# The opening of a hybrid RG-LRU / gMLP layer: decay series a term a round, spills on GpSimd's queue, another order of factors, rows and samples

## The reference

```
ada = silu(c) @ w_ada + b_ada            # nine vectors of 1024 for each of 9 sequences
h = x + 0.5 * g1 * SwiGLU1(mod(rms(x)))
h = h + gm * Mixer(mod(rms(h)))          # causal conv + RG-LRU, and a gMLP gating unit
h = h + 0.5 * g2 * SwiGLU2(mod(rms(h)))
y = mod(rms(h)) with shift, scale = silu(c) @ w_ada_final + b_ada_final
mod(v) = v * (1 + scale) + shift         # per sequence
```

## Time and profile before

| | us |
|---|---|
| median of 3 runs | 2403.04 |
| lowest, highest | 2400.04, 2405.37 |
| the profiled execution | 2404.43 |
| its span in the profile | 2402.7 |
| PE, DVE, ACT busy | 2342.3, 1579.6, 985.2 |

### The profile page before, as it was taken

How to read it: one execution, slowest core, us unless ns; L and a number is a source line. 1 busy time by engine, 2 the same in 40 slices (tenths; PEclk the granted TensorE clock), 3 DMA queues, 4 the chain that set the end, 5 groups by cost and what they waited for, 6 DMA issues and landing times.

```text
span 2402.7 us, 31657 instructions
## 1 busy us (share of the span) xinstructions
PE 2342.3 (97%) x11530; PEld 2007.2 (84%) x11530; DVE 1579.6 (66%) x2530; ACT 985.2 (41%) x1701; POOL 129.7 (5%) x173
## 2 busy tenths in 40 slices
PE   6999999999999999999999999999999999999998
PEld 4677777787788787999999999997777788878887
DVE  5965665666666766655666565569666666666667
ACT  4544444444233443443344434235444444433335
POOL 0010101100000000101011110000010100000000
PEclk8999999999999999999999999999999999999998
DMA  9465455548855332321222213423645533497642
GB/s 347 158 202 179 159 178 189 165 164 302 341 214 187 130 125 89 120 57 45 65 65 62 61 38 112 150 81 102 210 158 177 186 129 127 159 379 276 236 140 82
DMA packets 247342, 381.02 MB, mean 159 GB/s; under 512 B 16689, under 2 KB 158185, under 8 KB 246070
## 3 DMA queue, kind: packets, MB, share of 16 engines
q1 hardware_dynamic: 234526, 345.15, 41.7%
q0 software_dynamic: 10240, 33.56, 4.5%
q10 hardware_dynamic: 2456, 0.75, 0.1%
HBM read 262.93 MB, written 116.47 MB: 158 GB/s over the span
## 4 chain that ended last, share of the span: by engine, by line
PE 83%; DVE 8%; DMA 3%; issue 2%; ACT 2%; SPq 0%; DVEq 0%; ACTq 0%
PE bank L535 25%; PE bank L537 24%; PE bank L536 24%; PE bank L2931 2%; PE bank L2928 2%; PE bank L2930 2%; DMA wraw<-in_w_ffn_down 2%; DVE u_lo L629 1%; PE bank L2814 1%; PE bank L2844 1%; DVE wraw L656 1%; DVE x L2263 1%; DVE x L1909 1%; DMA xrow<-in_x_prompt 1%; DMA wraw<-in_w_ffn_up 1%
## 5 line engine op out<-in xcount | busy, mean ns | idle before, releaser
L535 PE MATMUL bank<-ops,u_hi 128*128 128x512 f32 x1232 | 489.2, 397 | 9.2 <-DVE ops L1942 4.0
L629 DVE TENSOR_TENSOR u_lo<-wraw,u_hi 128x512 fp32r<-128x512 f32 (+2 forms) x532 | 315.4, 618 | 277.3 <-ACT u_hi L623 274.9
L537 PE MATMUL bank<-ops,u_lo 128*128 128x512 f32 x1232 | 482.0, 391 | 0.0
L536 PE MATMUL bank<-ops,u_hi 128*128 128x512 f32 x1232 | 481.6, 391 | 0.0
L623 ACT ACTIVATE u_hi<-wraw 128x512 fp32r<-128x512 f32 (+2 forms) x532 | 287.4, 568 | 278.0 <-PE bank L537 167.8
L535 PE MATMUL bank<-xn_hi,w_hi 128*128 128x384 f32 x1104 | 370.5, 336 | 5.2 <-ACT ww L1689 2.0
L537 PE MATMUL bank<-xn_hi,w_lo 128*128 128x384 f32 x1104 | 369.6, 335 | 0.0
L536 PE MATMUL bank<-xn_lo,w_hi 128*128 128x384 f32 x1104 | 369.4, 335 | 0.0
L535 PEld LDWEIGHTS bank<-ops,u_hi 128*128 128x128 f32 x1232 | 232.6, 189 | 86.4 <-issue 23.4
L537 PEld LDWEIGHTS bank<-ops,u_lo 128*128 128x128 f32 x1232 | 232.5, 189 | 49.7
L536 PEld LDWEIGHTS bank<-ops,u_hi 128*128 128x128 f32 x1232 | 232.8, 189 | 46.5
(11 more groups left out here) (320 smaller groups left out, 3959.0 us busy)
## 6 DMA issues: line engine op xcount, KB each, us to landing
h_dram<-stage_hi SPq DMA_DIRECT2D x154, 256.0 KB, 2.4
h_dram<-stage_lo SPq DMA_DIRECT2D x154, 256.0 KB, 2.7
ada_in<-in_w_ada POOLq DMA_DIRECT2D x96, 256.0 KB, 3.7
raw<-in_w_in SPq DMA_DIRECT2D x48, 512.0 KB, 4.8
wraw<-in_w_ffn_gate SPq DMA_DIRECT2D x44, 512.0 KB, 4.8
wraw<-in_w_ffn_up SPq DMA_DIRECT2D x44, 512.0 KB, 4.9
wraw<-in_w_ffn_down SPq DMA_DIRECT2D x48, 384.0 KB, 5.2
x<-x_dram SPq DMA_DIRECT2D x6, 2304.0 KB, 9.4
```

Of the source, the lines that this page charges most:

```text
L535: nc.tensor.matmul(out, hi, mov_hi, start=first, stop=False, skip_group_check=True)
L536: nc.tensor.matmul(out, hi, mov_lo, start=False, stop=False, skip_group_check=True)
L537: return nc.tensor.matmul(out, lo, mov_hi, start=False, stop=last, skip_group_check=True)
L629: nc.vector.tensor_tensor(unit(u_lo, f, g, u, n), unit_source(u, n), unit(u_hi, f, g, u, n).bitcast(F32), ALU.subtract).then_inc(u_lo_read ...
```

## The change

VectorE's decay series is cut in pieces: `decay_begins` after round 1 of the first FFN, one `decay_term` after each of rounds 2 to 8, `decay_ends` after round 9; its buffer `spw` moves to a place of its own. The four input spills leave SP's queue for POOL's (with semaphores `x_kept`), and so do the gate-block loads, from ScalarE's. SP loads x tiles 6 to 8 without waiting for a spill, and weights ahead of modulation half 2. `first_rows(0)` and the fold of half 0 stand ahead of x tiles 3 to 5, the square root for tiles 0 to 3 after the fourth tile's squares; the factor's spread goes to bank 7 and ahead of `first_half(1)`. Units 1, 2, 3 are made later: unit 1 after B11's low part, units 2 and 3 after x tiles 6 to 8 on VectorE. The samples' first half stands ahead of T1 on all three engines, modulation halves 2 and 3 behind it on PE, half 3 behind T1's products. Units 8 and 9 stand ahead of 6 and 7. `made` is not changed.

```diff
@@ STAT
-    STAT = ((3, 4, 5), (6, 7, 5), (7, 7, 6), (6, 7, 5))
+    STAT = ((7, 4, 5), (6, 7, 5), (7, 7, 6), (6, 7, 5))
@@ SP
             weights(0, 0, 1, 0)
-            sp.wait_ge(x_in, 8)
-            spill(slice(0, KH), x_spilled, slice(0, PH))
             tile_rows(sp, 2)
-            ada_half(2)
             weights(0, 0, 0, 1)
             weights(0, 0, 1, 1)
+            ada_half(2)
             ada_half(3)
             sp.wait_ge(x_in, 2 * NT)
-            spill(slice(0, KH), x_spilled_late, slice(PH, TOK))
-            sp.wait_ge(x_spilled, 16)
-            spill(slice(KH, KT), x_spilled, slice(0, PH))
             sp.wait_ge(sumsq_mm, 9)
             ada_half(4)
-            sp.wait_ge(x_spilled_late, 16)
-            spill(slice(KH, KT), x_spilled_late, slice(PH, TOK))
@@ POOL
+            def spill_input(rows, cols, stored):
+                pool.dma_start(x_dram[:, rows, cols], x[:, rows, cols]).then_inc(stored, 16)
+            pool.wait_ge(x_in, 8)
+            spill_input(slice(0, KH), slice(0, PH), x_kept[0])
             pool.wait_ge(x_turned, 12)
             pool.wait_ge(sumsq_mm, 6)
             nc.gpsimd.memset(rg_sb[:, :, :, :], 0.0).then_inc(rg_zeroed, 1)
+            pool.wait_ge(x_in, 2 * NT)
+            spill_input(slice(0, KH), slice(PH, TOK), x_kept[1])
+            pool.wait_ge(x_kept[0], 16)
+            spill_input(slice(KH, KT), slice(0, PH), x_kept[0])
+            pool.wait_ge(x_kept[1], 16)
+            spill_input(slice(KH, KT), slice(PH, TOK), x_kept[1])
+            pool.wait_ge(rg_zeroed, 1)
...
+                    pool.dma_start(rg_sb[64 * h:64 * h + 64, :, gate, 64 * h:64 * h + 64], src)\
+                        .then_inc(rg_loaded, 16)
@@ ScalarE, before the rounds
-            row_squares(3, 6)
+            first_rows(0)
+            row_squares(3, 4)
             root(0, 0)
-            first_rows(0)
+            row_squares(4, 6)
             factor_copy(0, 0)
-            first_units(0)
+            unit_hi(act, 0, 0, 0)
             first_rows(1)
+            unit_hi(act, 0, 0, 1)
@@ ScalarE, opening_round
                     op_hi(f, O_B11)
+                    unit_hi(act, f, 0, 2)
+                    unit_hi(act, f, 0, 3)
                     row_squares(6, NT)
...
                     factor_copy(0, 2)
-                    act.wait_ge(rg_zeroed, 1)
-                    for gate, name in enumerate(("w_rg_a", "w_rg_x")):
...
+                    samples_hi(f, 0)
                     op_hi(f, O_T1)
                     first_rows(2)
-                    samples_hi(f, 0)
+                    unit_hi(act, f, 0, 8)
+                    unit_hi(act, f, 0, 9)
+                    first_rows(3)
+                    op_hi(f, O_B21)
                     unit_hi(act, f, 0, 6)
                     unit_hi(act, f, 0, 7)
-                    first_rows(3)
-                    unit_hi(act, f, 0, 8)
-                    unit_hi(act, f, 0, 9)
-                    op_hi(f, O_B21)
@@ VectorE, opening_round
+                    unit_lo(dve, f, 0, 2)
+                    unit_lo(dve, f, 0, 3)
                     weight_sum(dve, f, 0, 1)
                     weight_sum(dve, f, 0, 2)
                     unit_lo(dve, f, 0, 4)
                     unit_lo(dve, f, 0, 5)
+                    first_samples(0)
+                    first_samples_shifted(0)
+                    first_samples_lo(0)
                     for k in range(KH):
                         op_scale(f, k, 1)
                     for k in range(KH):
                         op_sum_(f, O_T1, k)
-                    first_samples(0)
-                    first_samples_shifted(0)
                     op_lo(f, O_T1)
-                    first_samples_lo(0)
-                    for i in range(3, 7):
-                        weight_sum(dve, f, 0, i)
                     first_half(2)
                     dve.wait_ge(ada_ready, 3)
                     scale_gain(SCALE1, KH, KT)
-                    unit_lo(dve, f, 0, 6)
-                    unit_lo(dve, f, 0, 7)
                     for k in range(KH):
                         op_scale(f, k + KH, 0)
-                    first_samples(1)
+                    for i in range(3, 7):
+                        weight_sum(dve, f, 0, i)
                     first_half(3)
                     dve.wait_ge(ada_ready, 4)
                     shift_difference(0)
                     unit_lo(dve, f, 0, 8)
                     unit_lo(dve, f, 0, 9)
                     op_lo(f, O_B21)
+                    unit_lo(dve, f, 0, 6)
+                    unit_lo(dve, f, 0, 7)
+                    first_samples(1)
                     first_samples_shifted(1)
@@ VectorE, after round_(g)
+                    if f == 0 and g == 1:
+                        decay_begins()
+                    elif f == 0 and g < 9:
+                        decay_term(17 - 2 * g)
+                    elif f == 0 and g == 9:
+                        decay_ends()
@@ VectorE, before the rounds
-            x_turned_in(1)
-            dve.wait_ge(x_in, 12)
-            reciprocal(0, 0)
             first_half(0)
             dve.wait_ge(ada_ready, 1)
             scale_gain(SCALE1, 0, KH)
-            for u in range(4):
-                unit_lo(dve, 0, 0, u)
+            x_turned_in(1, range(1))
+            reciprocal(0, 0)
+            x_turned_in(1, range(1, 3))
+            dve.wait_ge(x_in, 12)
             for k in range(KH):
                 op_scale(0, k, 0)
+            unit_lo(dve, 0, 0, 0)
             first_half(1)
             op_lo(0, O_B11)
+            unit_lo(dve, 0, 0, 1)
@@ PE
             first_half(0)
+            first_turn(0)
             x_turn(1)
-            first_turn(0)
-            def first_factors():
-                pe.wait_ge(x_in, 12)
-                spread(0, 0)
-            first_half(1, first_factors)
+            pe.wait_ge(ada_ready, 1)
+            spread(0, 0)
+            first_half(1)
             first_turn(1)
@@ PE, opening_round
                     spread(0, 2)
-                    first_half(2)
-                    first_half(3, lambda: first_turn(2))
                     pe.wait_ge(xs_lo_ready, 1)
                     samples_in(0, 0)
+                    pe.wait_ge(samples_act, FACTORS_MADE[0, 0])
+                    first_half(2)
+                    prompt(0, S1[0], O_T1, Z[0], True, False, True, lambda: first_turn(2))
+                    prompt(0, S1[1], O_T1, Z[1], True, False)
+                    first_half(3)
                     first_turn(3)
-                    prompt(0, S1[0], O_T1, Z[0], True, False, True)
-                    prompt(0, S1[1], O_T1, Z[1], True, False)
                     prompt(0, A12[0], O_B21, W[0], True, True, True)
```

More of the change, by code:

```diff
@@ L206, in build @@
     nrst = at("nrst", [P, 16])
+    spw = at("spw", [P, 6, KT])
     base = cursor[0]
@@ L364, in build @@
     hs_stored = sem("hs_stored")
+    x_kept = [sem(f"x_kept{i}") for i in range(2)]
     x_spilled = sem("x_spilled")
@@ L1091, in _ @@
             nc.gpsimd.memset(rg_sb[:, :, :, :], 0.0).then_inc(rg_zeroed, 1)
+            pool.wait_ge(x_in, 2 * NT)
[5 more added lines that the diff above has]
+            pool.wait_ge(rg_zeroed, 1)
+            for gate, name in enumerate(("w_rg_a", "w_rg_x")):
+                for h in range(2):
+                    src = ins[name].rearrange("o (k h) i j -> h i (o k) j", h=2)[h]
+                    pool.dma_start(rg_sb[64 * h:64 * h + 64, :, gate, 64 * h:64 * h + 64], src)\
+                        .then_inc(rg_loaded, 16)
             load_parts(0)
@@ L1194, in normalised, with first_units @@
                                      bias=prompt_scalar(SHIFTM, k)).then_inc(xn_hi_ready, 1)
-            def first_units(f):
-                for u in (EARLY if f == 1 else range(4)):
-                    unit_hi(act, f, 0, u)
+            def first_units():
+                for u in EARLY:
+                    unit_hi(act, 1, 0, u)
             def op_hi(f, o, tiles=slice(0, KH)):
@@ L1791, in _, with x_turned_in @@
                                     mybir.AxisListType.X, ALU.add)
-            def x_turned_in(t):
-                for s in range(3):
+            def x_turned_in(t, tiles=range(3)):
+                for s in tiles:
                     for b in range(2):
@@ L1820, in _, with decay_begins, decay_term @@
             step(nc.vector.scalar_tensor_tensor(spw[:, 0, :], lam, -1.0, lam, ALU.mult, ALU.max))
-            dve.wait_ge(sp_exp, 1)
-            step(nc.vector.tensor_scalar(spw[:, 2, :], spw[:, 1, :], 2.0, None, ALU.add))
-            after()
-            step(nc.vector.reciprocal(spw[:, 3, :], spw[:, 2, :]))
-            after()
-            step(nc.vector.tensor_tensor(spw[:, 0, :], spw[:, 1, :], spw[:, 3, :], ALU.mult))
-            after()
-            step(nc.vector.tensor_tensor(spw[:, 1, :], spw[:, 0, :], spw[:, 0, :], ALU.mult))
-            after()
```

(18 more changed lines are left out.)

38 lines of the change are left out of this document (17 added, 21 removed).

## The result

| | before | after |
|---|---|---|
| median, us | 2402.33 (5 runs) | 2414.94 (5 runs, 2413.26 to 2416.57) |
| the profiled execution | 2404.43 | 2413.26 |
| its span | 2402.7 | 2411.5 |

The ratio is 1.0048, 95% interval 1.0037 to 1.0058. Timed again beside other kernels (23 runs of before, 6 of after) it was 1.0058, 1.0045 to 1.0072. The change makes the kernel about 0.5% slower, 12 to 13 us. The prediction said slower, 2409.8, in a range from 2403.5 to 2416.0. The sign and the range hold. The size was some 5 us short: 6.8 us were forecast and 12.6 measured, and 2414.9 lies outside the narrower range, 2407 to 2412, that rival A had for itself. The profiled execution of after was the shortest of its five, so between the profiled ones the difference is only 8.8.

What follows compares the result with a forecast made beforehand. TensorE is busy 97% of the span, with VectorE beside it without slack behind the opening's first products. VectorE's new waits of 12.6 less 5.5 saved give 7.1, rounded to 6.8: median 2409.8 us, range 2403.5 to 2416.

Steps and rivals of the forecast that it cites:

- rival A: Opening: VectorE's new waits make the kernel slower, median 2409.8 us, own range 2407 to 2412; chance 0.50.
- Ninth unit: First round: `unit_lo(8)` waits by count for unit 6's high part; VectorE 3 us idle, PE some 8 before A12[0].
- First_half(3) behind T1: Behind T1's products: the fold of column 3 comes later, and VectorE waits 2.1 us for it.
- Fold of column 2: Opening, on VectorE: a new wait of 1.6 us for the fold of column 2.
- Samples' factor: Samples' chain ahead of T1: VectorE waits 2.9 us for the factor and 0.9 for their high part.
- A11[1] waits for unit_lo(2): After x tiles 6 to 8: PE idles from 41.7 to 44.7 us, the clock falls, A11[1] takes 4.3 instead of 2.85.
- Gate blocks: On POOL's queue behind the spills: landed by 77.8 us, just covered, cost 0; without cover 1 for 1.
- First spill on POOL: Before the first product: lands at 29.5 us, bounds 23.9 to 29.7, just hidden; later than 31 moves everything one for one.
- Late spill: Before T1: issued at 43.5 us, lands at 52, hidden; bounds 48.7 and 57, at 57 it costs 2.
- C: First spill crawls through POOL's queue, 14.8 us, landing at 36; first product at 41; + 13, 2416 us; chance 0.12.
- B's early product: Spill out of the way by 27 us, first product at 32.2, losses partly cancelled: 2407 us; chance 0.20.
- D's kept lead: The 6.7 us lead at T1 is kept, the counted waits and column 3's fold costing nothing: 2396.5 us; chance 0.09.

Runs made afterwards that it cites:

- the kernel with the new front and the old middle: Changed kernel, but spills on SP's queue and the kernel before's order from x tiles 6 to 8 on; gate blocks stay on POOL: 2406.40 us.
- the kernel with the middle alone: Kernel before with only the change's order from x tiles 6 to 8 to T2, spills and gate blocks where they were, `made` a plain count: 2411.46 us.

## Why the prediction was right, and where it was short

- *Ninth unit*, the step weighed most: right to a tenth in its size. Predicted 3 us of DVE idle and 8 of PE; measured 2.94 and 7.98, released by ScalarE's unit 6. Mending the count alone gave 3.7 of the mark back.
- *First_half(3) behind T1*: predicted a wait of 2.1, measured 1.81. *Fold of column 2*: 1.6 predicted, 0.78 measured. *Samples' factor* and its high part: 2.9 and 0.9 predicted, 1.24 and 0.70 measured.
- *A11[1] waits for unit_lo(2)*: predicted PE idle 3.0, measured 2.31. The clock was predicted to fall for it; it did not (0.40 us matmuls behind 48.61).
- *Gate blocks*: "just covered", right, though half 5 was loaded only at 94.5, later than its old use at 91.14; it was covered because the use had moved too, to 102.45. What the prediction missed is that the place of the blocks was safe only because the spills stood before them in the same list.
- *First spill on POOL* is the term that was mis-sized: 29.5 taken, 23.9 to 29.7 as bounds, 32.8 measured, outside the bounds and past the 31 us from which it decides. The upper bound was SP's own 8.5 us, the 11.7 measured is above it. The step that failed in it is "since the spill starts before": the prediction had the spill's bytes move from its issue on and delay the column half to 26.8. They waited 4.5 us for their first packet, and the column half, from which nothing had been taken by then, was taken up at 24.21. With A11[0] wholly at the low clock (5.26 us instead of the 4.2 taken) it makes the copies of x tiles 6 to 8 start at 44.15 instead of 39.7: 4.4.
- *Late spill*: "I take 52, hidden" was the other: 58.8, beyond the bound of 57, and DVE waits 2.60. It was issued 4.8 later than reckoned (48.25 for 43.5) and took 10.5 for 8.5.
- The terms together: predicted T2's sums at 86.7, measured 90.52. 4.4 + 2.6 on one side, 1.7 + 0.2 + 0.8 + 0.3 of the smaller waits on the other, make 4.0, where 3.8 were measured.
- *Decay series*: nothing in the rounds, right.
- The rivals. A's mechanism is what happened, but the total is outside A's own range. Of C, "the first spill crawls through POOL's queue", there was half: it took 11.7 us and not 14.8, and its sign, a first `op_scale` after 33, was missed by 0.14 us here (32.86) and met when after ran again (33.33). B's early product falls with the row at 32.86, D's kept lead with the one at 78.80. C was given 0.12 as if it excluded A; they added up, which is where some 4 of the 5 us are. That the range held is in part luck, as its upper end was C's price and not A's.
- Two small slips of the sum change nothing: the steps from 31.4 to the first product add up to 34.7 and not 35.0, and 2403 - 6.7 is 2396.3.
- The last us is not explained by the opening's order: the marks say 11 to 12, the totals 12 to 13, which is within the intervals. The 1.9 us that the profile of after gets back at the pause in front of round 1 is a peculiarity of the one profiled execution of before. In none of the thirteen other profiles does the clock fall there, and their later marks are 1.9 to 2.6 us lower against it. Whether most unprofiled executions of before keep the clock there too was not seen, but it would explain why totals follow the mark of round 0.

**The rule that was weighed.** The sum took nothing for GpSimd's descriptors starving under VectorE (the Trainium skill, SBUF — State Buffer, section "SBUF: two separate sides"). The late start is not this. In the kernel with the new front and the old middle the first gate block is issued by GpSimd at 25.99, and its first packet moves at 30.1, while VectorE stands idle from 24.3 on:

```profile
30.92 2.74 DVE L1921 SCALAR_TENSOR_TENSOR x<-x,ada,acc 128x512 f32<-128x512 f32 x4 [6.66 <-DMA x_dram<-x]
```

And the third spill of after starts 1.3 us after its issue although VectorE works without a pause from 59.26 on.

Another sentence of the skill is that a DMA engine goes round between the queues that have work, a packet at a time (DMA: Bandwidth & Descriptors, section "Queues, rings and completion order"). The trace agrees once the spill moves: 66 packets of GpSimd's queue and 65 of SP's in one microsecond, 67 and 65 in the next, 57 and 56 in the late spill. Halves of the packets are not halves of the bytes, since those of the spill are larger: from 26 to 28 us it got 270 GB/s. An estimate of 5.4 us for the spill, by half of some 390 GB/s from its issue on, fails at the start and not at the share. What holds the first packet of a spill back for 4.5 to 5.0 us beside SP's large loads, and for 1.3 to 1.5 us without them, is not shown. Full engines alone are not it: in the two microseconds after the late spill's issue SP's queue had 50 and 70% of them.

## What to carry to other kernels

- A transfer that others wait for didn't gain by a second queue beside a long series of loads: on GpSimd's it began to move 4.5 us after its issue and landed after 10.7 to 11.9 us (four profiles); on SP's, behind loads already queued, it landed after 6.0 to 9.8 (ten profiles). Before a rate is blamed for a late landing, the packets of each queue show whether it was slow or started late.
- When an order written by hand changes, look at what is waited for by count. A count waits for the slowest of all earlier items in the new order; here two pairs in swapped order cost 3.7 of the 11 us of the mark.
- An edit that moves cheap work away from a queue can set free what stood behind it. Taking the spills off POOL's list sent the gate blocks out 34 to 44 us sooner, into the fullest stretch, for 3 to 4 us. The late spill on SP's queue took 9.5 to 10.1 us in the three kernels with the blocks there and 5.1 to 6.7 in the seven without.

## What the runs showed of the hardware that I had not expected

- From the issue of a spill or gate block on GpSimd's queue to its first packet it took 4.1 to 5.0 us beside SP's large loads (twenty transfers in seven profiles) and 1.3 to 1.5 us behind them (fourteen transfers). Then the two queues alternated packet by packet.
- GpSimd issued each spill and gate block only as the one before had landed: in after the third spill, whose own wait had been met at 32.8, was issued at 59.02, 0.3 us after the late one's landing. The gate blocks went out every 3.0 to 3.1 us in a quiet stretch, every 6.5 us in a full one. This is not so for every transfer of this queue: at 111.36 it issued four loads of 256 KB within 2.2 us. What tells the two kinds apart was not tested.
- Issuing four DMAs of 128 KB from ScalarE while the engines are full took its list some 5 us (46.87 to 52.17 in the kernel with the middle alone): 0.69 us are marked for the first, 3.16 for the last two.
- The same 16 matmuls of a modulation half took 1.92, 3.31 or 3.64 us in the first 20 us of the span in different profiles, at a granted clock of 1.00, 0.56 and 0.50, and two kernels with the same code up to there (spills on SP, counts mended or not) have their first product at 35.71 and 36.36.
